# First weight group in contraction quarters beside the first token block, start of a hybrid decoder layer on 8 cores

## What is computed

```python
h    = rmsnorm(x, norm_pre)                          # (4, 4096, 2048)
proj = einsum('bsd,de->bse', h, w_in)                # 2048 -> 7168 columns
xa, ga, u, vb, gb, q, gc = split_cols(proj, IN_SPLITS)
ya = pool_mixer(xa, pool_w, pool_scale) * silu(ga)   # causal pooling, windows 2, 4, 8, 16
yb = spatial_gating(u, vb, ...) * silu(gb)           # per chunk of 128 tokens
yc = memory_cross_attention(q, k_m, v_m) * silu(gc)
y  = concatenate([rmsnorm(ya, g_a), rmsnorm(yb, g_b), rmsnorm(yc, g_c)])
x  = x + rmsnorm(einsum('bse,ed->bsd', y, w_out), norm_post)
```

## Time and profile before

| | us |
|---|---|
| median of 3 runs | 1270.57 (1270.1 to 1270.75) |
| profiled execution, its own time | 1267.24 |
| its span on the slowest core (core 3) | 1265.4 |
| PE busy | 1228.6 (97%) |
| spans of the 8 cores | 1259.8 to 1265.4 |

### The profile page before, as it was taken

The page is one execution under the profiler, slowest core; times in us unless marked ns, Lnnn a source line. Parts: engine busy times, 40 slices in busy tenths (PEclk is TensorE's granted clock), DMA queues, the critical chain, the costliest instruction groups (busy, mean ns, idle before and its releaser), DMA issues.

```text
span 1265.4 us, 17528 instructions; the slowest of 8 cores (1259.8 to 1265.4 us)
## 1 busy us (share of the span) xinstructions
PE 1228.6 (97%) x6258; PEld 573.7 (45%) x6258; DVE 529.3 (42%) x888; ACT 440.3 (35%) x811; POOL 151.0 (12%) x197
## 2 busy tenths in 40 slices
PE   5999999999999999999999999999999999999996
PEld 1444455444444444444444444444444444444442
DVE  3686654466344434432222232232323327322366
ACT  3566622122555444444222222222223222222222
POOL 0100231101010100101001010101010111222021
PEclk9999999999999999999999999999999999999999
DMA  8863499311999240404003403213173559994298
GB/s 198 209 216 134 62 169 148 62 28 20 183 166 161 41 67 1 67 1 67 1 1 53 81 6 63 36 32 67 34 135 65 100 87 150 159 170 67 37 186 245
DMA packets 31461, 119.40 MB, mean 94 GB/s; under 512 B 3152, under 2 KB 9552, under 8 KB 27344
## 3 DMA queue, kind: packets, MB, share of 16 engines
q0 software_dynamic: 22480, 76.03, 36.9%
q1 hardware_dynamic: 8896, 42.25, 13.1%
HBM read 164.93 MB, written 29.36 MB: 154 GB/s over the span
## 4 chain that ended last, share of the span: by engine, by line
PE 92%; DMA 4%; DVE 2%; issue 1%; ACT 1%; POOL 0%; SPq 0%; DVEq 0%; POOLq 0%; ACTq 0%
PE ps L380 91%; DMA arena<-wst 2%; DMA arena<-xT 2%; PE ps L938 1%; DVE arena L477 0%; PE ps L560 0%; DVE arena L613 0%; DVE arena L473 0%; DVE arena L619 0%; SPq L384 0%; DVE arena L1195 0%; POOL arena L387 0%; DVE arena L1253 0%; POOLq L1325 0%; DVE arena L634 0%
## 5 line engine op out<-in xcount | busy, mean ns | idle before, releaser
L380 PE MATMUL ps<-arena 128*128 128x512 bf16 (+3 forms) x5922 | 1222.6, 367 | 25.9 <-ACT arena L451 13.6
L380 PEld LDWEIGHTS ps<-arena 128*128 128x128 bf16 x5922 | 559.3, 98 | 666.2 <-issue 50.0
L535 ACT ACTIVATE arena<-arena 128x512 bf16<-128x512 f32 x96 | 68.8, 716 | 360.1 <-DVE arena L1087 173.7
L1195 DVE SCALAR_TENSOR_TENSOR arena<-ps,arena 128x512 f32<-128x512 f32 x128 | 95.7, 749 | 164.5 <-PE ps L380 158.9
L553 POOL TENSOR_TENSOR arena<-arena 128x512 bf16<-128x512 bf16 x44 | 53.0, 1206 | 587.8 <-ACT arena L538 495.2
L1199 ACT ACTIVATE ps<-arena 128x512 f32<-128x512 f32 x64 | 38.5, 601 | 220.8 <-PE ps L380 150.9
L387 POOL DMA_DIRECT2D arena<-wst x120 | 66.7, 571 | 313.5 <-PE ps L380 283.7
L1081 DVE SCALAR_TENSOR_TENSOR arena<-ps,arena 128x512 f32<-128x512 f32 x32 | 24.0, 751 | 155.4 <-PE ps L380 63.8
L613 DVE TENSOR_TENSOR arena<-arena 128x514 f32<-128x514 f32 (+5 forms) x72 | 55.2, 766 | 49.8 <-ACT arena L586 44.8
L885 DVE CAST arena<-ps 128x512 bf16<-128x512 f32 x32 | 22.1, 692 | 101.2 <-PE ps L380 93.9
L538 ACT ACTIVATE arena<-arena 128x512 bf16<-128x512 f32 x96 | 58.8, 613 | 0.0
(11 more groups left out here) (69 smaller groups left out, 419.3 us busy)
## 6 DMA issues: line engine op xcount, KB each, us to landing
arena<-wst POOLq DMA_DIRECT2D x120, 512.0 KB, 12.6
arena<-xT SPq DMA_DIRECT2D x16, 1024.0 KB, 12.0
out<-arena POOLq DMA_DIRECT2D x12, 1024.0 KB, 16.9
arena<-x SPq DMA_DIRECT2D x4, 1024.0 KB, 15.3
out<-arena SPq DMA_DIRECT2D x3, 1024.0 KB, 9.6
arena<-memT SPq DMA_DIRECT2D x2, 1024.0 KB, 6.4
arena<-norm_post SPq DMA_DIRECT2D x1, 1024.0 KB, 9.6
out<-arena SPq DMA_DIRECT2D x4, 256.0 KB, 2.2
```

The lines of the kernel that those rows point to most:

```text
L380: return lambda e: e.matmul(out, lhsT=lhsT, rhs=rhs, start=start, stop=stop)
L535: P.op("act", lambda e: e.activation(out=yT[:, c, tb * 512:(tb + 1) * 512], in_=tmp[ti][:], func=AF.Copy, scale=cp[:, CP_GBR + c:CP_GBR + ...
L1195: P.op("dve", lambda e: e.scalar_tensor_tensor(out=ra, in0=pv, scalar=sc(c), in1=ra, op0=ALU.mult, op1=ALU.add), reads=[bk(b), ("rbr", br) ...
```

## The change

`load_group(("A", 0), ...)` becomes four loads by contraction quarter: load `pc` holds the four steps of quarter `pc` for all four slots, packed so by the host (`first`), and goes to 4 slots x 1 KB per partition. They have no gate. x block 1 has no gate either and is issued right behind block 0; `poolw` and group 1 wait for the second piece of block 1 in place of the third. The small loads of `cp` and `xh` are issued by ACT in place of SP. PE starts with 22 matmuls on zeros, and block 0 is then projected quarter by quarter into four held banks, with the squares' sums between. Halo and pooling of group 0 move behind block 1, the silu of the raw gates moves into `unit(1, 0)`.

```diff
-    dma_sp(cp[:], cp_d, writes=["cp"], sem="d_c0")
-    dma_sp(xh[:].rearrange("p k t -> p (k t)"), xhT_d, writes=["xh"], sem="d_c1")
+    P.op("act", lambda e: e.dma_start(out=cp[:], in_=cp_d), writes=["cp"], dma_sem="d_c0")
+    P.op("act", lambda e: e.dma_start(out=xh[:].rearrange("p k t -> p (k t)"), in_=xhT_d), writes=["xh"],
+         dma_sem="d_c1")
     x0 = [load_x(0, pc) for pc in range(4)]
...
-    load_group(("A", 0), waits=[x0[2]])
+    for pc in range(4):
+        ks = range(pc * 4, pc * 4 + 4)
+        dma_pool(ring[:, 0:4, pc * 4:pc * 4 + 4, :].rearrange("p s k c -> p s (k c)"),
+                 w_d[CH[("A", 0, pc)]].rearrange("p (s n) -> p s n", s=4),
+                 writes=[M_ring(sl, ks) for sl in range(4)], sem=f"d_w{pc}")
...
+    x1 = [load_x(1, pc) for pc in range(4)]
+    dma_pool(poolw[:].rearrange("p g c d -> p (g c d)"), poolw_d, writes=[M_T], sem="d_c4", waits=[x1[1]])
+    load_group(("A", 1))
+
     norm_halo()
+    P.group("pe", [mm(psb(7), ones[:], sqx[1][:, 0:512], True, True) for _ in range(22)],
+            reads=[M_sqx[1], "ones"], writes=[bk(7)])
     sq0, sm0 = block_sums(0)
-    for i in range(8):
-        sq0(i)
-        x_raw(0, 2 * i)
-        x_raw(0, 2 * i + 1)
-        if i:
-            sm0(i - 1)
-    sm0(7)
-    x1 = [load_x(1, pc, waits=[wtok[("A", 0, 2)]] if pc == 0 else ()) for pc in range(4)]
-    dma_pool(poolw[:].rearrange("p g c d -> p (g c d)"), poolw_d, writes=[M_T], sem="d_c4", waits=[x1[2]])
-    load_group(("A", 1))
...
+    sq1, sm1 = block_sums(1)
+    bs0 = [bank(True) for _ in range(4)]
+    for pc in range(4):
+        sq0(2 * pc)
+        for k in range(pc * 4, pc * 4 + 4):
+            x_raw(0, k)
+        sq0(2 * pc + 1)
+        for s in range(4):
+            proj(s, 0, bs0[s], range(pc * 4, pc * 4 + 4))
+            if s > 1:
+                sm0(2 * pc + s - 2)
+
+    for k in range(4):
+        x_raw(1, k)
     for s in range(4):
-        b = bank()
-        proj(s, 0, b)
-        if s < 2:
-            a_halo(0, s)
-            xa_evict(0, s, 0, b, True)
-            a_chain(0, s, 0)
-        else:
-            if s == 3:
-                for k in range(4):
-                    x_raw(1, k)
-            gate_evict(0, s - 2, b, True, 0)
+        (xa_evict if s < 2 else gate_mul)(*((0, s, 0, bs0[s], True) if s < 2 else (0, s - 2, bs0[s], 0)))
+    release(*bs0)
...
+    for cc in range(2):
+        a_halo(0, cc)
+        a_chain(0, cc, 0)
```

More of the change, by code:

```diff
@@ L304, in M_ytile, with M_ring @@
         return Mem(*[(YA + c * 4 * KB + t * 256, 256) for c in range(c0, c0 + 8)])
-    def M_ring(s):
-        return Mem((RG + s * 4 * KB, 4 * KB))
+    def M_ring(s, ks=range(16)):
+        return Mem((RG + s * 4 * KB + ks[0] * 256, len(ks) * 256))
     M_tmp = [Mem((o_tmp[i], 2 * KB)) for i in range(2)]
@@ L429, in build_program @@
     P.op("dve", lambda e: e.memset(ones[:], 1.0), writes=["ones"])
+    P.op("dve", lambda e: e.memset(sqx[1][:, 0:512], 0.0), writes=[M_sqx[1]])
     P.op("dve", lambda e: e.memset(stat[:], 0.0), writes=["stat"])
@@ L522, in proj @@
                        for k in ks],
-                reads=[M_ring(slot), M_hT(tb, ks)], writes=[bk(b)])
+                reads=[M_ring(slot, ks), M_hT(tb, ks)], writes=[bk(b)])
     late = []
@@ L630, in a_chain, with gate_mul, gate_act @@
             P.op("dve", lambda e: e.tensor_copy(out=X_[:, 0:16], in_=X_[:, 512:528]), reads=[MX], writes=[MX])
[L632 to L637, removed]
-        else:
-            silu(b, ts + dc)
+    def gate_mul(tb, dc, b, ts):
+        P.op("dve", lambda e: e.tensor_tensor(out=tmp[ts + dc][:], in0=psb(b), in1=rst[tb][:], op=ALU.mult),
+             reads=[bk(b), M_rst[tb]], writes=[M_tmp[ts + dc]])
+    def gate_act(i):
+        P.op("act", lambda e: e.activation(out=tmp[i][:], in_=tmp[i][:], func=AF.Silu),
+             reads=[M_tmp[i]], writes=[M_tmp[i]])
     def pool_part(g, tb, ts):
@@ L654, in pool_part, with a_block @@
         pair_ss(0, tb, g == 0, g == 3)
[L656 to L663, removed]
+    def a_block(g, tb):
         r0 = halves[("A", g)] * 4
@@ L670, in a_block @@
                 a_halo(g, cc)
-            xa_evict(g, cc, tb, b, raw)
+            xa_evict(g, cc, tb, b, False)
             a_chain(g, cc, tb)
-            pump(n[cc])
             if cc == 0:
@@ L678, in a_block @@
             proj(r0 + 2 + dc, tb, b)
-            gate_evict(tb, dc, b, raw, ts)
-            pump(n[2 + dc])
+            silu(b, ts + dc)
         late.append(lambda: pool_part(g, tb, ts))
@@ L729, in build_program @@
                 x_raw(1, k, "dve" if k % 4 < 2 else "act")
-            sm1(2 * pc - 2)
-            sm1(2 * pc - 1)
         sq1(2 * pc)
         sq1(2 * pc + 1)
-        for k in range(pc * 4, pc * 4 + 4):
-            x_norm(0, k)
+        for k in range(pc * 4 - 4, pc * 4):
+            if k >= 0:
+                x_norm(0, k)
         for s in range(4):
             proj(s, 1, bs[s], range(pc * 4, pc * 4 + 4))
+            if s > 1:
+                sm1(2 * pc + s - 2)
+    for k in range(12, 16):
+        x_norm(0, k)
     for pc in range(4):
@@ L743, in build_program @@
                                           op0=ALU.mult), reads=[M_T], writes=[M_T])
-    sm1(6)
-    sm1(7)
+    for cc in range(2):
+        a_halo(0, cc)
+        a_chain(0, cc, 0)
     def unit(g, tb, at, chain=True):
@@ L765, in unit @@
             else:
-                gate_evict(tb, s - 2, b, False, ts)
+                silu(b, ts + s - 2)
             do(2 * s + 1)
@@ L784, in stream @@
         for s in range(2):
-            gate_evict(tb, s, bs[2 + s], False, ts)
+            silu(bs[2 + s], ts + s)
         release(*bs)
@@ L795, in gates1 @@
         for dc in range(2):
-            gate_evict(1, dc, bs[2 + dc], True, 2)
+            gate_mul(1, dc, bs[2 + dc], 2)
         release(*bs)
@@ L804, in build_program @@
     unit(1, 0, {0: [C(xa_evict, 0, cc, 1, bs[cc], True) for cc in range(2)] + [gates1],
-                2: N(1, 0, 3), 3: [C(pp, 0, 0)], 4: N(1, 3, 6) + [C(a_chain, 0, cc, 1) for cc in range(2)],
+                2: N(1, 0, 3) + [C(gate_act, i) for i in range(4)], 3: [C(pp, 0, 0)], 4: N(1, 3, 6) + [C(a_chain, 0, cc, 1) for cc in range(2)],
                 6: N(1, 6, 9) + [C(a_chain, 1, 0, 0), C(sq2, 0), C(sq2, 1)],
@@ L1345, in _pack_weights @@
     wst = np.empty((NCH, 128, 2048), np.float32)
+    first = [w_in[:, c:c + 128].reshape(4, 4, 128, 128) for c in (C_XA, C_XA + 128, C_GA, C_GA + 128)]
     for g in range(4):
@@ L1354, in _pack_weights @@
             wst[CH[("B", g, 2 * s + 1)]] = _slot(w_in[:, C_U + c:C_U + c + 128])
+    for pc in range(4):
+        wst[CH[("A", 0, pc)]] = np.stack([w[pc].transpose(1, 0, 2).reshape(128, 512) for w in first],
+                                         axis=1).reshape(128, 2048)
     for hf in range(2):
```

2 lines of the change are left out of this document (removed).

## The result

| | us |
|---|---|
| median of 7 runs, changed kernel | 1277.03 |
| median of 7 runs, kernel before | 1270.57 |
| ratio | 1.0055, interval 1.0045 to 1.0066 |
| profiled execution after, its own time | 1278.5 |
| spans of the 8 cores after | 1268.4 to 1276.8, mean 1272.7 |

The changed kernel is slower by 5.7 to 8.4 us, 7.0 at the middle of the interval. One run of the seven of each kernel (1378.28 and 1341.35 us) lies far above its others and stays out of the ratio. The two profiled executions lie further apart (1278.5 against 1267.24) than the medians: that of before is near the low end of its runs (1266.78) and that of after above the median of its own. So I compare stages, and take means over the eight cores where a stage differs between them.

A forecast was written before the change was run, and what follows sets the result against it. PE, 92% of the last chain, bounds the kernel, so its idle or slow time near the start counts. Block 1's end +4.6, halo +1.1, pause -1.3: total +4.5 on median 1270.57, likeliest 1275.0, range 1269.0 to 1280.0.

The forecast's parts named there:

- rival (a): Loads at the start: queues share packet by packet, slower by 4.5 us; chance 0.68 that it is over 0.2%.
- Turns, one row each: Two busy queues at the start: an engine takes one packet of each in turn, whatever the sizes.
- (b): Weight queue gets half the engines' time: fourth load at 33.5, -4.0 us, about 1266.6; chance 0.12.
- (c): Two weight packets per turn beside block 0: load at 38.7, +1.2; chance 0.20 together with rival (a)'s cheap end.
- The 13 weight rows against 8: Turns beside x block 0: 52 weight packets would pass, the fourth load 2.0 us sooner.
- Fourth weight load at 42.0 (40 to 44): Group 0's last quarter lands at 4.9 + 13.0 + 14.3 + 9.8 = 42.0; weight price ends give 40.0 to 44.0.
- First weights at 21.5, `xh` near 13, zeros end at 24: Start of block 0: halo load, then matmuls on zeros until 24, covered by the weight loads, only just.
- Last quarter 4.4 us, slow restart taken as 0: Block 0's 20 matmuls behind the fourth load take 4.4 us; slow clock costed 0, 1.7 kept for the range.
- Its bound of 1.7: Slow start of block 0's last quarter: at most 4.15 - 11 x 0.22 = 1.7 us.
- Block 1 18.04 us: Block 1's 80 matmuls take 17.74 us as before, plus 0.3 for waiting on evictions, ends 0 and 2.8.
- The base: End of block 1 before, taken as 59.79; against it 64.4 was forecast, +4.6.
- Behind it, -0.2: Behind block 1: 32 moved halo matmuls +1.1, the pause of 1.26 at 68.28 gone, -1.3.

The follow-up runs named there:

- e8: Kernel before, with only the gate of weight group 0 taken off; 1278.03 us, ratio 1.0081.
- e6: Changed kernel without the 22 matmuls on zeros ahead of block 0; 1275.75 us, ratio 1.0058.
- e1: Changed kernel with x block 1 again held back until the third weight load has landed; 1271.63 us, ratio 0.9993.
- e11: Changed kernel with 8 more matmuls on zeros between the third and fourth quarter of block 0; 1274.8 us, ratio 1.0052.
- e7: Kernel before, with only the gate of x block 1 taken off; 1273.7 us, ratio 1.0033.
- e9: Changed kernel with 4 KB weight rows, small loads first on SP, poolw and group 1 behind x block 1's third piece; 1267.64 us, ratio 0.9981.
- e12: e9 with block 0's matmuls of a quarter issued step by step across the four slots; 1263.93 us, ratio 0.9972.
- e3: Changed kernel with only the small loads cp and xh back on SP, ahead of x block 0; 1275.08 us, ratio 1.0044.
- e4: Changed kernel with 16 more matmuls on zeros between the third and fourth quarter of block 0; 1281.18 us, ratio 1.0064.
- e2: Changed kernel with weight group 0 laid out by quarter, one 4 KB run per partition, gates still off; 1272.94 us, ratio 1.0007.

## Why the prediction held, and what was sized wrong

The call (slower, by rival (a)) and its mechanism were right; 1277.03 lies 2.0 us above 1275.0. At the stage itself the forecast was 4.2 us short, +4.6 in place of +8.8, so that the time came this near is in part luck. By its steps:

- **Turns, one row each.** Right for 1 KB against 8 KB, 1 KB against 2 KB and 4 KB against 2 KB (changed kernel) and for 4 KB against 8 KB (e8). Rivals (b) and (c) fall: the fourth load landed at 41.0 to 43.6, not at 33.5 or 38.7. Its evidence was weaker than it says: of the two places of the earlier trace rows the second has 1.40 MB against 0.52, so 2.7 to 1 in bytes, not the reverse of 16 to 1; the equal counts stand. The Trainium skill, page "DMA: Bandwidth & Descriptors", section "Queues, rings and completion order", gives typically about 9 to 17 descriptors per turn. The 13 weight rows against 8 that the prediction tried by it would have given, by estimate, 350 against some 215 in 8 to 19 us and the fourth load at 40.0; 328 passed, and no core had the load before 41.0. Turns of several rows, equal on both sides, would give the same counts as single rows and are not excluded.
- **Fourth weight load at 42.0 (40 to 44).** It landed at 42.5 in the mean; PE's wait for it ended at 41.2 to 43.9, mean 42.7. The start may be what is missing, which no run isolates: the first weight packet ran at 6.3 to 7.7 us, 4.6 us or more behind the issue at 1.62, where the sum starts at 4.9.
- **First weights at 21.5, `xh` near 13, zeros end at 24.** 22.4 in the mean, 12.7 to 13.9, and 24.0 on core 2 (ACT's squares, which wait for the zeros, start at 24.02). The zeros chain was covered, as costed; e6 and e1 show both sides of that cover.
- **Last quarter 4.4 us, slow restart taken as 0.** This is the term that was mis-sized: 6.05 in the mean, so 1.7 in place of 0, and up to 3.0 on one core. The prediction took the 1.47 us pause of the earlier trace rows as its evidence that a pause is free, although it had itself worked out gaps between landings of 6.8 us with 4.4 us of work. The real last pause was 2.2 to 4.2 us, and behind it the granted clock read 0.50 (core 2); e11 showed that the loss goes with the pause. Its bound of 1.7 was too low as well, since it took the slow stretch as 11 matmuls, and core 2 shows 12 in 44 to 48 us alone.
- **Block 1 18.04 us.** 18.5. The pause for the eviction was 0.79 where 0.3 had been taken.
- **The base.** The 59.79 of the earlier trace rows was core 3, the slowest; the mean over cores, without the table load, was 58.5. So the end of block 1 moved by 8.8 us (67.31 against 58.53) where 4.6 had been said: 0.7 from the load, 1.7 from the clock, 0.4 from block 1, 1.3 from the base, which makes up the 4.2 but for rounding.
- **Behind it, -0.2.** -0.4 (third Ln 8.4 later). The table load and the pause went as said.

The measured ratio, 7.0 us, is less than the 8.4 of the means at block 2. That remains open: a mean over cores of one execution is compared with the slowest core of many.

The prediction costed the gate of x block 1 only through the weights' turns in the new layout. e7 shows that it is worth 4 us in the kernel before as well, with 2 us of a later start of the transfers in it; neither forecast had a term for that.

## What to carry to other kernels

When two queues are busy, count rows, not bytes: here a load in rows of 1 KB got an eighth of the bytes of one in rows of 8 KB beside it. Give the load that is needed first the longest rows, or hold its partner back with a gate; here either was worth 6 to 8 us. Long rows do not replace the right order of work: e8, with 4 KB weight rows beside x block 0 in the old order, lost 10 us. In this kernel the work in quarters paid once the x piece and the weights of a quarter arrived together (e9), and then the first operation behind each landing was what to shorten (e12).

## What was not expected of the hardware

- Pauses of PE of about 2 to 4.2 us were followed by a slow quarter on some cores and not on others: 2.06 was in e3 (core 3, 6.26 us for the quarter), 2.97 was not in e6 (core 0, 4.57). The 3 us that the expectation of e4 names as the border is not one.
- In the first slow stretch of the changed kernel (core 2, 18 to 22 us) matmuls run one each 0.43 us, while the profile's clock reads 1.00.
- POOL issued the first weights at 1.6 us in all kernels without their gate. With four runs per partition the first packet ran at 5.3 to 8.2 us, whichever queue had the small loads. With one run it ran at 3.0 to 3.4 where SP had the small loads (e8, e9, e12) and at 6.0 to 7.3 where ACT had them (e2). The reason is open, as is that of the start about 2 us later in e7.
